# Closing a layer: the middle tile's residual sum on TensorE and ScalarE, stored in halves

## The reference

```python
f = moe(h.reshape(B * T, D), ...)               # routed experts plus one shared expert
x = x + gate_f * rmsnorm(f, g_post_ffn)         # x: the residual stream after the mixers
```

## Time and profile before

| | us |
|---|---|
| median of 3 runs | 743.12 |
| lowest and highest | 740.5, 745.71 |
| profiled execution, its own time | 742.79 |
| its span, first to last instruction | 741.0 |
| TensorE busy in the span | 693.1 (94%) |
| DVE busy | 391.8 (53%) |
| ScalarE busy | 191.0 (26%) |
| moved by the transfer engines | 259.14 MB, mean 350 GB/s |
| mean granted TensorE clock | 0.979 |

### The profile page before, as it was taken

One profiled execution on the slowest core, in us unless ns is written; L12 is line 12 of the kernel. 1 busy time (PEld: TensorE's weight loads), 2 busy tenths in 40 slices (PEclk: granted clock), 3 DMA queues, 4 the chain that ended last, 5 costly groups with the idle time before them and its releaser, 6 DMA issues.

```text
span 741.0 us, 11368 instructions
## 1 busy us (share of the span) xinstructions
PE 693.1 (94%) x4209; PEld 402.8 (54%) x4209; DVE 391.8 (53%) x1002; ACT 191.0 (26%) x321; POOL 82.3 (11%) x47
## 2 busy tenths in 40 slices
PE   1799999899999999999999999999799999998993
PEld 1689788677866735545445554444345445443441
DVE  3388999685285564454434545454435446332214
ACT  3244332763372202211111111112111211110113
POOL 2445544503300100000000000000000000000000
PEclk9899999989999999999999999999989999999998
DMA  9999766905489478799999999999999999999993
GB/s 319 373 333 336 247 228 228 331 11 170 144 327 426 185 305 351 309 359 425 425 425 421 428 425 424 425 424 424 425 429 422 427 422 427 425 424 421 418 397 125
DMA packets 51004, 259.14 MB, mean 350 GB/s; under 512 B 6656, under 2 KB 9312, under 8 KB 32896
## 3 DMA queue, kind: packets, MB, share of 16 engines
q1 hardware_dynamic: 46816, 252.50, 84.7%
q0 software_dynamic: 1520, 4.87, 1.9%
q10 hardware_dynamic: 2608, 1.00, 0.5%
HBM read 254.64 MB, written 3.71 MB: 349 GB/s over the span
## 4 chain that ended last, share of the span: by engine, by line
PE 78%; DMA 14%; DVE 3%; SPq 2%; ACT 1%; issue 1%; POOL 0%; ACTq 0%; DVEq 0%
PE psum L2237 23%; DMA w_gu<-in_w_expert_gu 12%; PE psum L2245 10%; PE psum L2131 8%; PE psum L2209 7%; PE psum L550 5%; PE psum L552 5%; PE psum L551 5%; PE psum L2112 3%; DMA w_gu<-in_w_ada 2%; PE psum L2143 1%; PE psum L1867 1%; PE psum L2351 1%; PE psum L2196 1%; SPq L684 1%
## 5 line engine op out<-in xcount | busy, mean ns | idle before, releaser
L2237 PE MATMUL psum<-w_gu,hgT 128*32 128x512 f32 (+1 forms) x1280 | 195.4, 608 | 7.5 <-DMA w_gu<-in_w_expert_gu 7.5
L2237 PEld LDWEIGHTS psum<-w_gu,hgT 128*32 128x32 f32 (+1 forms) x1280 | 58.5, 121 | 136.0 <-issue 135.9
L1674 DVE TENSOR_TENSOR f_acc<-f_acc,psum 128x512 f32<-128x512 f32 x132 | 86.7, 684 | 43.3 <-PE psum L2209 43.3
L2245 PE MATMUL psum<-w_dn,actT 128*32 128x512 f32 (+1 forms) x640 | 98.5, 596 | 0.5 <-ACT actT L1035 0.5
L1652 DVE SCALAR_TENSOR_TENSOR act<-sil,wsl,psum 128x256 f32<-128x256 f32 x27 | 18.4, 680 | 138.2 <-ACT sil L1060 133.0
L535 POOL TENSOR_TENSOR w_lo<-w_gu,w_hi 128x2048 fp32r<-128x2048 f32 x13 | 59.8, 4597 | 76.4 <-ACT w_hi L829 76.4
L2131 PE MATMUL psum<-onehot,h_lo 128*128 128x512 f32 (+1 forms) x168 | 66.6, 397 | 0.0
L2131 PE MATMUL psum<-onehot,h_hi 128*128 128x512 f32 (+1 forms) x168 | 64.9, 386 | 0.0
L1658 DVE TENSOR_TENSOR y_lo<-psum,y_hi 128x1024 fp32r<-128x1024 f32 x26 | 31.8, 1224 | 50.4 <-ACT y_hi L1064 50.4
L1060 ACT ACTIVATE sil<-psum 128x256 f32<-128x256 f32 x27 | 10.4, 385 | 185.7 <-PE psum L2237 185.7
L2245 PEld LDWEIGHTS psum<-w_dn,actT 128*32 128x32 f32 (+1 forms) x640 | 27.0, 119 | 57.3 <-issue 56.6
(11 more groups left out here) (307 smaller groups left out, 865.4 us busy)
## 6 DMA issues: line engine op xcount, KB each, us to landing
w_gu<-in_w_expert_gu SPq DMA_DIRECT2D x49, 2048.0 KB, 21.1
w_dn<-in_w_expert_down SPq DMA_DIRECT2D x61, 1024.0 KB, 19.3
w_gu<-in_w_expert_gu SPq DMA_DIRECT2D x27, 1024.0 KB, 12.0
w_gu<-in_w_ada SPq DMA_DIRECT2D x12, 2048.0 KB, 13.8
w_gu<-in_w_in SPq DMA_DIRECT2D x4, 2048.0 KB, 12.7
w_gu<-in_w_out SPq DMA_DIRECT2D x2, 2048.0 KB, 10.0
bc<-mod_rows POOLq DMA_DIRECT2D x6, 512.0 KB, 7.4
w_gu<-in_w_expert_gu SPq DMA_DIRECT2D x6, 512.0 KB, 20.4
```

The costliest lines, as they stand in the source:

```text
L1674: v.tensor_tensor(dst, dst, bank(5 + n), ALU.add).then_inc(f_added, 1)
L2237: ins = t.matmul(bank(target)[rows, :], column(c)[:, rows], w_gu[s][:, c, :], start=(c == 0), stop=(c == NC - 1), tile_position=(0, rows.s ...
L2245: ins = t.matmul(bank(target + n)[rows, :], actT[:, j, rows], w_dn[s][:, j, 512 * n:512 * (n + 1)], start=(j == 0), stop=(j == 1), tile_po ...
```

## The change

TensorE gets four more products at the end of its program, into banks 2 and 3, which are free by then: for each half of the columns of tile 1, identity times x (as soon as x is back), and then a diagonal matrix of rstd times the gated tile, added in the same bank. The result in the bank is the same sum that the fused instruction on DVE made. DVE builds the diagonal (`rstd_diag`, the identity times the per-partition value rstd) where it used to compute tile 1's result. ScalarE copies each bank over x when its second product is done (`scaled`). The two halves of the middle tile are stored by themselves, and SP waits for `y_mid` and `y_last` where it waited for `y_out`. The other side of the branch gets the stores in halves as well, but keeps its arithmetic on DVE.

```diff
--- before.py
+++ after.py
@@ -291,6 +291,7 @@
         comb = at("comb", [P, NT, NE], BC + 21760)
         onehot_over = at("onehot_over", [P, NT, P], Z + 40960, F32R)
         last_sq = at("last_sq", [P, D], BC)
+        rstd_diag = at("rstd_diag", [P, P], BC + 8192)
         last_t = [at("last_t0", [P, D], BC + 4096), at("last_t1", [P, D], Z + 24576), at("last_t2", [P, D], Z + 36864)]
 
 
@@ -367,6 +368,8 @@
         gu_first = [sem(f"gu_first{s}") for s in range(SLOTS)]
         gu_in = [sem(f"gu_in{s}") for s in range(SLOTS)]
         dn_in = [sem(f"dn_in{s}") for s in range(SLOTS)]
+        y_mid, y_last = sem("y_mid"), sem("y_last")
+        diag_ready, scaled = sem("diag_ready"), sem("scaled")
         gu_third, dn_first = sem("gu_third"), sem("dn_first")
         gu_used = [sem(f"gu_used{s}") for s in range(SLOTS)]
         dn_used = [sem(f"dn_used{s}") for s in range(SLOTS)]
@@ -790,15 +793,14 @@
                             sp.nop()
             with sp.Else():
                 sp.nop()
-            for i in range(NT - 1):
-                sp.wait_ge(y_out, i + 1)
-                dst = t_out[0][0] if i == 0 else t_out[1][0, P * (i - 1):P * i, :]
-                sp.dma_start(dst, x[:, i, :]).then_inc(out_sem, 16)
-            for n in range(2):
-                cols = slice(512 * n, 512 * (n + 1))
-                sp.wait_ge(y_out, NT + n)
-                sp.dma_start(t_out[1][0, P * (NT - 2):P * (NT - 1), cols], x[:, NT - 1, cols]).then_inc(out_sem, 16)
-            sp.wait_ge(out_sem, 16 * (NT + 3))
+            sp.wait_ge(y_out, 1)
+            sp.dma_start(t_out[0][0], x[:, 0, :]).then_inc(out_sem, 16)
+            for i in range(1, NT):
+                for n in range(2):
+                    cols = slice(512 * n, 512 * (n + 1))
+                    sp.wait_ge(y_last if i == NT - 1 else y_mid, n + 1)
+                    sp.dma_start(t_out[1][0, P * (i - 1):P * i, cols], x[:, i, cols]).then_inc(out_sem, 16)
+            sp.wait_ge(out_sem, 16 * (2 + 2 * NT - 1))
             sp.wait_ge(m_out, 32)
 
 
@@ -1125,6 +1127,9 @@
                 for i in range(NT):
                     a.wait_ge(gated_ready, i + 1)
                     squares(i, bank(TOTAL_BANK[2 * i], 0, 1024))
+                for n in range(2):
+                    a.wait_ge(scaled, n + 1)
+                    a.activation(x[:, 1, 512 * n:512 * (n + 1)], bank(Y_CLOSING + n), ACT.Copy).then_inc(y_mid, 1)
             with a.Else():
                 own.count = branch_count
                 for k in range(LAST, GROUPS):
@@ -1760,9 +1765,21 @@
                 v.wait_ge(fsq, i + 1)
                 v.wait_ge(gated_ready, i + 1)
                 own.link(v.reciprocal(rstd[:, i:i + 1], sum_sq[:, i:i + 1]))
-                for cols in [slice(0, D)] if i < NT - 1 else [slice(0, 512), slice(512, D)]:
+                for cols in [slice(0, D)] if i == 0 else [slice(0, 512), slice(512, D)]:
                     v.scalar_tensor_tensor(x[:, i, cols], last_t[i][:, cols], rstd[:, i:i + 1], x[:, i, cols],
-                                           ALU.mult, ALU.add).then_inc(y_out, 1)
+                                           ALU.mult, ALU.add).then_inc((y_out, y_mid, y_last)[i], 1)
+
+            def closing_two(sources):
+                v.wait_ge(gate_rows_in, 32)
+                v.wait_ge(x_back, 16 * NT)
+                gated(0, sources[0])
+                gated(1, sources[1])
+                gated(2, sources[2])
+                result(0)
+                v.wait_ge(fsq, 2)
+                own.link(v.reciprocal(rstd[:, 1:2], sum_sq[:, 1:2]))
+                v.tensor_scalar(rstd_diag[:, :], ident, rstd[:, 1:2], None, ALU.mult).then_inc(diag_ready, 1)
+                result(2)
 
             def closing(sources):
                 v.wait_ge(gate_rows_in, 32)
@@ -1780,7 +1797,7 @@
                 for k in range(LAST, GROUPS):
                     group_closing(k)
                 low_y_halves(Y_CLOSING)
-                closing(TOTAL_BANK[0::2])
+                closing_two(TOTAL_BANK[0::2])
             with v.Else():
                 own.count = branch_count
                 for k in range(LAST, GROUPS):
@@ -2448,6 +2465,14 @@
                         ins = total_part(2 * i + n, k % 2, y_lo, True)
                         if n:
                             ins.then_inc(total_done, 1)
+                t.wait_ge(x_back, 16 * NT)
+                for n in range(2):
+                    t.matmul(bank(Y_CLOSING + n), ident, x[:, 1, 512 * n:512 * (n + 1)], start=True, stop=False)
+                t.wait_ge(diag_ready, 1)
+                t.wait_ge(gated_ready, 2)
+                for n in range(2):
+                    t.matmul(bank(Y_CLOSING + n), rstd_diag[:, :], last_t[1][:, 512 * n:512 * (n + 1)],
+                             start=False, stop=True).then_inc(scaled, 1)
 
             assert len(BATCHES[NB - 1]) == BATCH
             for k in range(LAST):
```

## The result

The changed kernel took 746.45 us in the median of 20 executions against 743.9 for 20 of the kernel before: a ratio of 1.0032, 95% interval 1.0017 to 1.0048, or 2.4 us (1.3 to 3.6). Its profiled execution took 745.89 us with a span of 744.1. The forecast was 745.4 and no change by the 1% bound.

What follows compares the result with a forecast made beforehand. The end was taken as the first store's start plus an unbroken stream of stores. Late middle-tile stores at full clock add 0.9 us, at half clock 2.6 in all; 742.79 + 2.6 = 745.4 us, range 741.4 to 748.2.

Steps and rivals of the forecast that it cites:

- no change by the 1% bound: Whole kernel: differences within about 1%, 7.4 us, count as the same; chance of same 0.96.
- The identity products are free: TensorE after the last sums: four records from about 729.3 to 731.2 us while it was idle; their wait for x costs nothing.
- DVE gains 0.73 us: DVE's end: tile 1's 1.28 us replaced by a 0.28 us multiply, last halves ending 0.73 us earlier.
- The gain can't be used: SP's stores: the last tile's ready halves wait behind the middle tile's second half; the store stream bounds the end.
- Half clock: TensorE's diagonal products: clock fallen to half after 3.3 us idle, making the end +2.6 us instead of +0.9; chance 0.45.
- The size: Whole kernel: 2.6 us slower, with the span ending at 743.58 us instead of 741.0.
- The time itself: Whole kernel: profiled execution of 742.79 us plus 2.6 gives 745.4 us.
- A late instruction: Rival, ends of TensorE's and ScalarE's programs: code still to be fetched, some 2 us per stall, up to 747.4; chance 0.10.
- The stream's fixed end: After the store stream: the span ends a constant 1.95 us behind the stream's end.
- The best that any version can do: Rival, store stream: no hole, so no change at 742.8 us, also the best possible for this change; chance 0.04.
- The rule on a store's time: Last store: 2.0 us plus bytes over 436 GB/s, 2.6 us for 256 KB; would make the difference 2.5 instead of 2.6 us.

Runs made afterwards that it cites:

- the three traces named above: Traces of both edits, first tile in halves and all tiles in halves; DVE's first product waited for reloaded x; tails 12.32, 11.91 and 11.08 us.
- the two others with the same gap: Changed kernel executed again unedited, and changed kernel with SP storing the last tile's halves before the middle tile's; tails 15.08 and 12.59 us.
- the repeat: The changed kernel profiled again with no edit; tail 15.08 us against 14.82, ratio to the kernel before 1.0023 (1.0002 to 1.0043).
- split only: Changed kernel with tile 1's result back on DVE in two instructions, stored in halves, no added products or copies; tail 11.62 us, one execution.
- all tiles in halves: Kernel before with all three tiles' results on DVE in halves of 512 columns, six stores; tail 11.08 us, ratio 0.9995 (0.9982 to 1.0008).
- first tile in halves: Kernel before with tile 0's result made on DVE and stored in two halves; tail 11.91 us, ratio 1.0013 (0.9992 to 1.0033).
- no middle result: Kernel before without tile 1's result, x stored as it was reloaded; tail 11.74 us against 11.83, one execution.
- both edits: Changed kernel with the last tile's halves stored first and TensorE kept at work up to the diagonal; tail 12.32 us, ratio 1.0003 (0.9984 to 1.0022).

## Why the prediction was right

- **The identity products are free.** Right: 729.45 to 731.33, under DVE's work. That the wait for x costs nothing held for this trace and the one before; in the three traces named above x came up to 0.6 us late.
- **DVE gains 0.73 us.** Right: 2.16 us from the first store's issue to its end instead of 2.89. The 128x128 multiply took 0.29 (taken as 0.28).
- **The gain can't be used.** Right, and for both reasons given: SP's order (storing the last tile first returned 2.2 us, 1.0 of them in the landing) and the stream of stores (leaving the middle tile's result out returned 0.1).
- **Half clock.** Right, from the rows in which most falls came sooner than 3.3 us into a gap, and with some luck: it had a chance of 0.45. The clock fell 3.1 us into the gap in the first profiled run, 0.16 us before the products; the products ran at half again in the two others with the same gap, and at full where the gap was filled or cut to 1.57 us. The first product took 2.07 us against 1.87 priced: the weight loads went slower as well, 0.34 us against 0.19. In the first run the clock came back 3.3 us after the work began and shortened the last record, which made up for that; in the two others it stayed at half.
- **The size.** 2.6 us forecast; 3.0 in the tails, 2.55 between the medians, 2.4 (1.3 to 3.6) by the ratio. The close agreement of the medians is luck. None of the excess in the tails is on TensorE: the second copy ended 4.64 us after the first store's issue, 4.63 forecast. It is all behind that copy, 5.27 us instead of 4.87: 0.1 until the data flowed again, 0.1 in the length of the stream, 0.2 behind it. In the repeat the second copy came 0.2 us later (4.84), with the clock at half to the end.
- **The time itself.** 745.4 stood on one execution of 742.79 us; the median of 20 is 743.9, and 743.9 + 2.6 = 746.5 against 746.45 measured.
- **A late instruction.** Given 0.10; no engine stopped for one: TensorE began 0.05 us after the diagonal, the second copy 0.04 us after the last product, and no table load came ahead of the copies. But the tail does move code: queues named "instruction" carry a few packets in every trace, and q8 among them only in the six with the new path. In the rows below (packets, MB, share of the 16 engines' time) the first two are the changed kernel's, the third is from the split only. Whether these packets delay the stores on the shared engines is open.

```profile
q8 instruction: 2, 0.03, 1.2%
q14 instruction: 3, 0.02, 0.8%
...
q14 instruction: 3, 0.02, 0.9%
```

- **The stream's fixed end.** Mis-sized as a constant of 1.95 us: from the end of the dense stream to the end of the span it was 2.15 in the changed kernel, 1.4 with all tiles in halves and 1.15 with the last tile stored first. It has two parts in the traces. The last packets of the stores go singly behind the stream: for 0.2 us with the last tile first, 0.8 in the kernel before, 1.25 in the changed one. From the last of them to the end of the span it is 0.8 to 1.15 us in all eleven traces. The first part is what varies most.
- **"The best that any version can do"** for a stream without a hole, 742.8, was wrong: it took the stream's start as given. With the first tile in halves the data flows 5.22 us after DVE's start in both traces, 5.75 in all the others, and with halves throughout the tail went 0.75 us under that of before. That the whole kernel gains by it is not shown.
- **The rule on a store's time.** The Trainium skill (DMA: Bandwidth & Descriptors, Anatomy of one DMA) gives its fit, 2.0 us plus bytes over 436 GB/s, for transfers that GpSimd issues; the prediction used it for stores that SP issues and did not say so. Worked out from it as an estimate, half a tile takes 2.6 us. With halves throughout, the four later stores landed after 2.5 to 2.7 us, near it; behind a queue half a tile took up to 4.3 us (no middle result), which it leaves out.

## What to carry to other kernels

Before moving work off the engine that ends last, ask what that engine feeds: here the stores were already one unbroken stream, and 0.73 us saved on DVE was worth about 0.1. A short burst of TensorE work behind a gap of some 3 us ran at 1.2 GHz, but for the end of it in one, in three profiled runs out of three; either price it so or keep the engine at work up to it. And put the result that takes the longest path last in a queue that waits in order.

## What was not expected of the hardware

- A store's landing went with what was queued ahead of it: half a tile (256 KB) landed 2.0 to 2.4 us after its issue at the head of the stream, 2.5 to 2.7 when DVE fed the queue at its own pace, and up to 3.6 (before, changed), 3.9 (both edits) and 4.3 (no middle result) behind other stores.
- The issue of one more store on a queue that already holds some can take two to three times as long: 0.79 us in the changed kernel, 0.92 in its repeat, 0.86 with both edits, 0.82 without the middle result, where most take 0.33.

```profile
L802 SPq DMA_DIRECT2D out<-x x4: 332/398/788, 737.3 to 740.1; - x4
...
L804 SPq DMA_DIRECT2D out<-x x4: 332/332/332, 735.4 to 737.6; - x4
...
DMA to landing us min/median/max: 2.5/2.6/2.7
```

The first row is the changed kernel's, the other two are those with all tiles in halves. Why these issues were slow is open.
